# Decode attention in a hybrid decoder step: each partition subtracts its own maximum, the maximum across partitions is taken once per step, and the decode blocks pass two at a time

## What is computed

```python
def fox_attention(q, k, v, cq, ck, q_pos, k_pos):
    ...
        s = jnp.einsum('bqhd,bkhd->bhqk', q_blk, k,
                       preferred_element_type=jnp.float32) * scale
        s = s + (cq_blk[..., :, None] - ck_t[:, :, None, :])
        mask = k_pos[None, :] <= p_blk[:, None]
        s = jnp.where(mask, s, NEG_BIG)
        p = jax.nn.softmax(s, axis=-1)
        return jnp.einsum('bhqk,bkhd->bqhd', p.astype(v.dtype), v)
```

## Time and profile before

| | us |
|---|---|
| median of 3 runs | 1908.2 |
| lowest and highest | 1907.0, 1912.0 |
| the profiled execution | 1911.6 |
| its span, first to last instruction | 1910.0 |
| `fox` in it | about 130 to 745 |

### The profile page before, as it was taken

The page is one execution under the profiler, slowest core; times in us unless marked ns, Lnnn a source line. Parts: engine busy times, 40 slices in busy tenths (PEclk is TensorE's granted clock), DMA queues, the critical chain, the costliest instruction groups (busy, mean ns, idle before and its releaser), DMA issues. The chain is left out here.

```text
span 1910.0 us, 30732 instructions
## 1 busy us (share of the span) xinstructions
PE 1664.6 (87%) x10909; PEld 1571.7 (82%) x10909; DVE 933.8 (49%) x1794; ACT 684.5 (36%) x1089; POOL 541.0 (28%) x340
## 2 busy tenths in 40 slices
PE   4498797898799653898994999999999999999997
PEld 4487686787688532896993999999999999999997
DVE  6425537646646554537324545444444444544444
ACT  3323543553453441224234333222222222445344
POOL 4411222232223111623300222222222222544541
PEclk6699999899899865998996999999999999999999
DMA  3324244244243224400005431111111111211122
GB/s 102 117 75 133 70 136 137 80 135 134 67 145 115 69 96 160 175 1 25 23 1 216 133 100 44 44 44 47 52 44 44 44 49 50 106 51 45 45 67 89
DMA packets 211045, 158.16 MB, mean 83 GB/s; under 512 B 23201, under 2 KB 199233, under 8 KB 209872
## 3 DMA queue, kind: packets, MB, share of 16 engines
q1 hardware_dynamic: 168492, 120.48, 20.3%
q10 hardware_dynamic: 41656, 31.92, 5.5%
q0 software_dynamic: 784, 4.31, 0.6%
HBM read 123.95 MB, written 32.89 MB: 82 GB/s over the span
## 5 line engine op out<-in xcount | busy, mean ns | idle before, releaser
L176 PE MATMUL ps<-x_hi,w_hi 128*128 128x344 f32 x1584 | 508.3, 321 | 1.1 <-issue 1.1
L177 PE MATMUL ps<-x_lo,w_hi 128*128 128x344 f32 x1584 | 505.7, 319 | 0.0
L178 PE MATMUL ps<-x_hi,w_lo 128*128 128x344 f32 x1584 | 505.6, 319 | 0.0
L176 PEld LDWEIGHTS ps<-x_hi,w_hi 128*128 128x128 f32 x1584 | 297.6, 188 | 3.0 <-issue 1.4
L178 PEld LDWEIGHTS ps<-x_hi,w_lo 128*128 128x128 f32 x1584 | 298.0, 188 | 0.0
L177 PEld LDWEIGHTS ps<-x_lo,w_hi 128*128 128x128 f32 x1584 | 297.3, 188 | 0.1
L176 PE MATMUL ps<-h_hi,wm_hi 128*128 128x344 f32 x672 | 226.8, 337 | 0.2
L177 PE MATMUL ps<-h_lo,wm_hi 128*128 128x344 f32 x672 | 218.7, 325 | 0.0
L178 PE MATMUL ps<-h_hi,wm_lo 128*128 128x344 f32 x672 | 218.4, 325 | 0.0
L2284 POOL TENSOR_TENSOR w_lo<-w_raw,w_hi 128x1024 fp32r<-128x1024 f32 x42 | 110.1, 2621 | 371.2 <-ACT w_hi L2452 371.2
L2288 POOL TENSOR_TENSOR w_lo<-w_raw,w_hi 128x512 fp32r<-128x512 f32 x44 | 112.1, 2554 | 134.7 <-ACT w_hi L2495 134.7
(11 more groups left out here) (366 smaller groups left out, 2908.7 us busy)
## 6 DMA issues: line engine op xcount, KB each, us to landing
w_raw<-in_w_up SPq DMA_DIRECT2D x44, 512.0 KB, 3.9
k_past<-in_cache_k SPq DMA_DIRECT2D x256, 64.0 KB, 1.9
v_past<-in_cache_v SPq DMA_DIRECT2D x256, 64.0 KB, 2.0
wm_raw<-in_w_in ACTq DMA_DIRECT2D x28, 512.0 KB, 4.1
w_raw<-in_w_down SPq DMA_DIRECT2D x44, 256.0 KB, 2.7
gdn_scratch<-conv ACTq DMA_DIRECT2D x12, 528.0 KB, 3.1
g_qkv<-gdn_scratch SPq DMA_DIRECT2D x12, 528.0 KB, 9.9
x_scratch<-xT POOLq DMA_DIRECT2D x1, 4128.0 KB, 11.4
```

Source lines behind the costliest of these rows:

```text
L176: pe.matmul(out, w_hi, a_hi, start=first, stop=False)
L177: pe.matmul(out, w_hi, a_lo, start=False, stop=False)
L178: return pe.matmul(out, w_lo, a_hi, start=False, stop=last)
```

## The change

The subtraction of the maximum across partitions is taken out of each block. Each partition ("lane") subtracts its own maximum over the 8 pages (`lane_max`) right after the scores, in the same slot; the exponential follows in the same slot, the weighing one slot later, the page sums two slots later, into a tile `v_sum` that keeps the sums of all eight sequences of a step. In slot 0 of the next step POOL takes one maximum across partitions, 16 columns wide; DVE turns it into a factor for each lane, head and sequence (`factor_logs`), ACT exponentiates these factors (`exp_factors`, slot 1), DVE multiplies the lanes' sums of probabilities with them (`lane_weights`, slot 2), and PE sums over partitions in nine matmuls (`past_values`, slot 2): one for the denominators, and one for each sequence whose weights are `v_sum` and whose two columns are the factors. `dec_result` in slot 3 reads them from PSUM. `v_past` has 2 buffers instead of 3, and SP's load of a block waits for the page sums two blocks back.

The diff without the declarations of tiles and semaphores:

```diff
@@ fox: tiles
-        v_past = sb("v_past", [P, 3, PAGES, P])
+        v_past = sb("v_past", [P, 2, PAGES, P])
+        v_sum = sb("v_sum", [P, DEC, P])
...
@@ SP
             def load_v(n, pages):
-                need(sp, dval_done, 0, n - 2)
+                need(sp, v_summed, 0, n - 1)
                 settle(sp, "sp")
-                load_past(n, v_past[:, n % 3], t["cache_v"], pages, v_loaded[n % 3])
+                load_past(n, v_past[:, n % 2], t["cache_v"], pages, v_loaded[n % 2])
...
@@ PE
-            def past_values(n):
-
-                need(pe, v_summed, 0, n + 1)
-                need(pe, dval_out, 0, n)
-                if n % DEC == DEC // 2:
-                    need(pe, normed, n // DEC, 1)
-                pe.matmul(ps[:, 7, 0:16], v.ones[:], score[:, n % DEC].rearrange("p g h -> p (g h)"), start=True, stop=True)
-                pe.matmul(ps[:, 7, 16:17], v_past[:, n % 3, 0], v.ones[:, 0:1], start=True, stop=True).then_inc(dval_done.sem, 1)
+            def past_values(j):
+
+                need(pe, den_ready, j, 1)
+                need(pe, v_summed, j, DEC)
+                need(pe, normed, j, 1)
+                pe.matmul(ps[:, 7, 0:2 * DEC], v.ones[:], lane_sum.rearrange("p b h -> p (b h)"), start=True, stop=True)
+                for b in range(DEC):
+                    mm = pe.matmul(ps[:, 7, 2 * DEC + 2 * b:2 * DEC + 2 * b + 2], v_sum[:, b], lane_factor[:, b], start=True, stop=True)
+                mm.then_inc(dval_done.sem, 1)
...
                 l2_sums(j, i, 1)
-                if NBLK * j + i >= VALUES_AFTER:
-                    past_values(NBLK * j + i - VALUES_AFTER)
+                if j and i == 2:
+                    past_values(j - 1)
                 turn_probs(j, i, 1)
...
@@ ACT
                 need(act, dsub_ready, 0, n + 1)
-                act.activation(score[:, b], score[:, b], ACT.Exp)
-                act.activation(d_pself[:, j % 2, b], d_self[:, j % 2, b], ACT.Exp).then_inc(dexp.sem, 1)
+                act.activation(score[:, b], score[:, b], ACT.Exp).then_inc(dexp.sem, 1)
+
+            def exp_factors(j):
+                need(act, fsub_ready, j, 1)
+                act.activation(factors, factors, ACT.Exp).then_inc(factors_ready.sem, 1)
...
                         slot(j, i)
-                    n = NBLK * j + i - 1
-                    if 0 <= n < PAST:
-                        exp_decode(n)
+                        exp_decode(NBLK * j + i)
+                    if j and i == 1:
+                        exp_factors(j - 1)
...
@@ POOL
-            def all_max(n):
-                b = n % DEC
-                need(pool, dmax_ready, 0, n + 1)
+            def all_max(j):
+                need(pool, dsub_ready, j, DEC)
                 settle(pool, "pool")
-                pool.partition_all_reduce(d_all[:, b], d_max[:, b], P, RMAX).then_inc(dmax_all.sem, 1)
+                pool.partition_all_reduce(d_all.rearrange("p b h -> p (b h)"), lane_max[:, j % 2].rearrange("p b h -> p (b h)"), P, RMAX).then_inc(dmax_all.sem, 1)
...
                     n = NBLK * j + i
-                    if 0 <= n - 1 < PAST:
-                        all_max(n - 1)
+                    if j and i == 0:
+                        all_max(j - 1)
...
-                    if 0 <= n - 2 < PAST:
-                        weigh(n - 2)
+                    if 0 <= n - 1 < PAST:
+                        weigh(n - 1)
...
@@ DVE
-                dve.tensor_reduce(d_max[:, b], score[:, b].rearrange("p g h -> p h g"), AX.X, ALU.max).then_inc(dmax_ready.sem, 1)
-
-            def dec_less_max(n):
-                j, b = divmod(n, DEC)
-                need(dve, dmax_all, 0, n + 1)
-                dve.tensor_tensor(d_max[:, b], d_all[:, b], d_self[:, j % 2, b], ALU.max)
+                top = lane_max[:, j % 2, b]
+                dve.tensor_reduce(top, score[:, b].rearrange("p g h -> p h g"), AX.X, ALU.max)
                 dve.drain()
-                dve.tensor_tensor(score[:, b], score[:, b], d_max[:, b].unsqueeze(1).broadcast_to([P, PAGES, 2]), ALU.subtract)
-                dve.tensor_tensor(d_self[:, j % 2, b], d_self[:, j % 2, b], d_max[:, b], ALU.subtract).then_inc(dsub_ready.sem, 1)
+                dve.tensor_tensor(score[:, b], score[:, b], top.unsqueeze(1).broadcast_to([P, PAGES, 2]), ALU.subtract).then_inc(dsub_ready.sem, 1)
 
             def sum_pages(n):
 
                 need(dve, v_weighed, 0, n + 1)
-                vb = v_past[:, n % 3]
...
-            def past_out(n):
-                need(dve, dval_done, 0, n + 1)
-                b = n % DEC
-                dve.tensor_copy(dden[:, 16 * b:16 * b + 16], ps[:, 7, 0:16])
-                dve.tensor_copy(dnum[:, b:b + 1], ps[:, 7, 16:17]).then_inc(dval_out.sem, 1)
+                need(dve, dval_done, n // DEC, 0)
+                vb = v_past[:, n % 2]
...
+                dve.tensor_tensor(v_sum[:, n % DEC], vb[:, 0], vb[:, 1], ALU.add).then_inc(v_summed.sem, 1)
+
+            def lane_sums(j):
+                need(dve, dexp, j, DEC)
+                dve.tensor_reduce(lane_sum, score.rearrange("p b g h -> p b h g"), AX.X, ALU.add)
+
+            def factor_logs(j):
+                need(dve, dmax_all, j, 1)
+                dve.tensor_tensor(d_all, d_all, d_self[:, j % 2], ALU.max)
+                dve.drain()
+                dve.tensor_tensor(lane_factor, lane_max[:, j % 2], d_all, ALU.subtract)
+                dve.tensor_tensor(self_factor, d_self[:, j % 2], d_all, ALU.subtract).then_inc(fsub_ready.sem, 1)
+
+            def lane_weights(j):
+                need(dve, factors_ready, j, 1)
+                dve.tensor_tensor(lane_sum, lane_sum, lane_factor, ALU.mult).then_inc(den_ready.sem, 1)
...
                         normalise(j - 1)
+                        lane_sums(j - 1)
+                    if j and i == 2:
+                        lane_weights(j - 1)
                     if j < STEPS:
                         dec_score(j, i)
...
-                    if 0 <= n - 1 < PAST:
-                        dec_less_max(n - 1)
-                    if 0 <= n - VALUES_AFTER < PAST:
-                        past_out(n - VALUES_AFTER)
-                    if 0 <= n - 3 < PAST:
-                        sum_pages(n - 3)
+                    if 0 <= n - 2 < PAST:
+                        sum_pages(n - 2)
...
-                    if i == 3 and j:
+                    if j and i == 0:
+                        factor_logs(j - 1)
+                    if j and i == 3:
                         dec_result(j - 1)
```

More of the change, by code:

```diff
@@ L825, in fox @@
         score = sm(2 * DEC * PAGES).rearrange("p (b g h) -> p b g h", b=DEC, g=PAGES)
-        dden = sm(2 * DEC * PAGES)
-        d_max, d_all, d_den = (sm(2 * DEC).rearrange("p (b h) -> p b h", b=DEC) for _ in range(3))
-        d_self, d_pself = (sm(4 * DEC).rearrange("p (n b h) -> p n b h", n=2, b=DEC) for _ in range(2))
-        qk_self, dnum, d_tmp = sm(DEC), sm(DEC), sm(DEC)
+        lane_sum, d_all, d_den = (sm(2 * DEC).rearrange("p (b h) -> p b h", b=DEC) for _ in range(3))
+        d_self, lane_max, factors = (sm(4 * DEC).rearrange("p (n b h) -> p n b h", n=2, b=DEC) for _ in range(3))
+        lane_factor, self_factor = factors[:, 0], factors[:, 1]
+        qk_self, d_tmp = sm(DEC), sm(DEC)
         q_dec, k_dec = sm(DEC), sm(DEC)
@@ L849, in fox @@
         k_loaded = [count(f"kpast_loaded{i}", 0) for i in range(2)]
-        v_loaded = [count(f"vpast_loaded{i}", 0) for i in range(3)]
-        k_used, dmax_ready, dmax_all, dsub_ready, dexp = (count(n, DEC) for n in ("kpast_used", "dmax_ready", "dmax_all", "dsub_ready", "dexp"))
-        v_weighed, v_summed, dval_done, dval_out = (count(n, DEC) for n in ("v_weighed", "v_summed", "dval_done", "dval_out"))
+        v_loaded = [count(f"vpast_loaded{i}", 0) for i in range(2)]
+        k_used, dsub_ready, dexp, v_weighed, v_summed = (count(n, DEC) for n in ("kpast_used", "dsub_ready", "dexp", "v_weighed", "v_summed"))
+        dmax_all, fsub_ready, factors_ready, den_ready, dval_done = (count(n, 1) for n in ("dmax_all", "fsub_ready", "factors_ready", "den_ready", "dval_done"))
         dec_out, dec_stored = count("dec_out", 1), count("dec_stored", 16)
@@ L1391, in sum_pages @@
-                for m in (4, 2, 1):
-                    ins = dve.tensor_tensor(vb[:, 0:m], vb[:, 0:m], vb[:, m:2 * m], ALU.add)
-                    if m > 1:
-                        dve.drain()
-                ins.then_inc(v_summed.sem, 1)
-            def past_out(n):
-                need(dve, dval_done, 0, n + 1)
-                b = n % DEC
-                dve.tensor_copy(dden[:, 16 * b:16 * b + 16], ps[:, 7, 0:16])
-                dve.tensor_copy(dnum[:, b:b + 1], ps[:, 7, 16:17]).then_inc(dval_out.sem, 1)
@@ L1403, in dec_result @@
-            def dec_result(j):
-                need(dve, dexp, j, DEC)
-                dve.drain()
-                dve.tensor_reduce(d_den, dden.rearrange("p (b g h) -> p b h g", b=DEC, g=PAGES), AX.X, ALU.add)
-                dve.drain()
```

(7 more changed lines are left out.)

20 lines of the change are left out of this document (11 added, 9 removed).

## The result

The changed kernel takes 1880.1 us (median of 4 runs, 1875.8 to 1886.0) beside 1908.3 for the kernel before: 0.986 of it (95% interval 0.984 to 0.988), by this ratio 27 us faster. I had forecast 1830 and a range from 1803 to 1866, so the sign is right and the size is not: the change brought a third of the 78 us. Another run of the same kernel gave 0.985 (0.983 to 0.987).

What follows compares the result with a forecast made beforehand. GpSimd's queue, filled by all-reduces of 13.5 us, was taken to pace VectorE and through it a nearly full TensorE. Terms -50 - 19 + 5 - 2 - 12 = -78 us gave 1830 us, range 1803 to 1866.

Steps and rivals of the forecast that it cites:

- Item 1: TensorE's waits for VectorE's probabilities copy and score rounds, 58.2 us in the four steps, mostly go: -50 us (-58 to -43).
- the first places: Slots 2 to 3 of each step, where TensorE waits for copy and score round; 2 us left at each of four.
- the second ones: Slots 4 to 5 of each step, the other place of TensorE's waits for VectorE; nothing left there.
- Item 2: Seven stretches of TensorE work at half clock, 42.9 us, return to 2.4 GHz: -19 us (-21 to -10).
- Item 3: TensorE's l2 sums, reached earlier, wait longer for ScalarE's squares in half of the places: +5 us (0 to +10).
- Item 4: Values' matmuls within the steps fall from 10 to 6 us; about half lost to the transpose's copy wait: -2 us.
- Item 5: Tail after step 3: one all-reduce in line instead of three, decode result earlier: -12 us (-16 to -8).
- the signs that I had named: Prediction wrong if first-place holes stay above 5 us, GpSimd waits for values' loads, or all-reduce results take over 10 us.
- The unknown call: The all-reduce over 16 columns, not in the trace: taken at 13.5 us as for 2 columns; upper bound 108 us.
- The slower rival: The all-reduce grows with its columns; at 108 us a call the kernel takes 2190 us; chance 0.04.
- VectorE takes GpSimd's place: VectorE, about as full as TensorE in slots 1 to 3, binds; items 1 and 2 give 36: 1863 us; chance 0.20.
- the ring of two: With two values buffers loads come too late in short slots; GpSimd waits, 45 us given back: 1875 us; chance 0.04.

Runs made afterwards that it cites:

- after_again: The changed kernel itself, nothing altered, run again for comparison with other kernels on the same chip; 0.985 of the kernel before.
- no_reads: Changed kernel with GpSimd's weighing, weight split and mask tile all replaced by fills of the same tiles; 0.960 of the kernel before.
- no_reduce: Changed kernel with its four remaining all-reduces replaced by a GpSimd copy of 16 columns; 0.981 of the kernel before.
- v_first: Changed kernel with SP issuing a block's values ahead of the keys two blocks on instead of behind them; 0.981 of the kernel before.
- weigh_memset: Changed kernel with GpSimd filling a block's values with ones where it weighed them; 0.971 of the kernel before.

## Why the prediction was wrong

**What bounds the kernel.** Right: TensorE's idle time and clock are what could be won, and GpSimd's queue did pace VectorE. The release came: VectorE's 88.0 us of waiting are gone.

**Item 1, -50.** This term failed. Copy and score rounds together went from 62.1 to 27.2 us. Without the tail's 3.9, which item 1 left out, that is from 58.2 to 27.2 us, -31. At the first places, where I had left 2 us each, TensorE waits 5.8, 1.2, 3.8 and 3.8 us (step 0's hole had been 4.3 us, not the 10.7 that I took for all, and grew); at the second ones, where I had left nothing, 3.1 to 3.2 us in every step. The step that failed is the one with which I gave "nothing at the second ones" and 2 us at the first: I took VectorE's durations from rows in which GpSimd was in the silent stretch of an all-reduce (taps 4.09, sums 1.55) and kept them for a GpSimd that no longer stands still. The second place of step 1 shows it. Before, it was 3.0 us:

```profile
367.78 1.65 PE L967 MATMUL ps<-kT,qT 64*128 64x384 f32 x4 [3.04 <-DVE fox_small L1342]
```

After, it is 3.06 us, and VectorE's sums ahead of it take 3.18 and 1.84 us instead of 1.55 in all, beside split and weighing:

```profile
346.05 3.18 DVE L1391 TENSOR_TENSOR v_past<-v_past 128x512 f32<-128x512 f32 x2
349.30 1.84 DVE L1393 TENSOR_TENSOR v_sum<-v_past 128x128 f32<-128x128 f32 x1
...
346.30 2.64 POOL L730 TENSOR_TENSOR wm_lo<-wm_raw,wm_hi 128x1024 fp32r<-128x1024 f32 x1 [11.31 <-ACT wm_hi L726]
348.90 2.08 POOL L1302 TENSOR_TENSOR v_past<-v_past,fox_small 128x1024 f32<-128x1024 f32 x1
...
356.93 0.92 PE L967 MATMUL ps<-kT,qT 64*128 64x384 f32 x4 [3.06 <-DVE fox_small L1345]
```

Without GpSimd's reads the two waits are 7.3 us, -51: the size that I had.

**Item 2, -19.** TensorE was busy 10 us less in this profile and 0.6 less in that of `after_again`, at the same idle time (91.0 and 89.3); in `no_reads` 23 less, which is what items 2 and 4 take off its busy time together (19 and 4). The clock comes back where the holes go, and here half of them stayed.

**Item 3, +5.** It was +0.7, after and in `no_reads`. **Item 4, -2.** The wait of the transposes for their copies, which I had called half lost, grew from 13.2 to 20.3 us, and the collected matmuls wait 5.2 us in slot 2 of steps 1 to 3, where I had named the cover and priced it at nothing: together 12 us more, of which my sum had 2.

**Item 5, -12.** Right in size: from the start of the last decode scores to the next stage 35.1 us instead of 48.0, from their end to the decode result 28.7 us, where I had said 28: the end of the last block's subtraction and of the result's last product are

```profile
674.57 0.17 DVE L1383 TENSOR_TENSOR fox_small<-fox_small 128x16 f32<-128x16 f32 x1
...
703.25 0.16 DVE L1424 TENSOR_TENSOR fox_small<-fox_small 64x8 f32<-64x8 f32 x1
```

The all-reduce in it is worth less than I thought (3.6 us, `no_reduce`).

**The sum.** This profile is 36 us shorter instead of 78: item 1 brought 19 us too little, TensorE's busy time (items 2 and 4) 13, and the waits of item 4 took 10 more than I had; item 3 came out 4 us better, and the next stage lost 4. Two of the signs that I had named came: a first place above 5 us, in step 0, and GpSimd waiting for the values' loads.

**The unknown call.** The all-reduce over 16 columns has about the cost of the one over 2, as taken; my estimate of 1.7 us more for the columns does not show in the recorded part (0.39 us for 0.37):

```profile
419.51 0.39 POOL L1307 PARTITION_ALL_REDUCE fox_small<-fox_small  x1 [5.96 <-issue]
```

Behind the four calls 6.8 to 7.7 us follow without a record. The slower rival is out.

**The rivals.** "VectorE takes GpSimd's place" was the right one, with "if sums and weighings collide more than now" as its condition; it had 0.20 and a time of 1863. It was too low in both, since I priced only the first places. The condition stood in my own rows: the product with the keys takes 1.22 us in one slot and 2.01 in the next, with no other shape; the second one begins while a weight split still runs, and the weighing behind that split takes 2.88 instead of 1.89 us:

```profile
313.93 2.38 POOL L730 TENSOR_TENSOR wm_lo<-wm_raw,wm_hi 128x1024 fp32r<-128x1024 f32 x1
316.27 2.88 POOL L1298 TENSOR_TENSOR v_past<-v_past,fox_small 128x1024 f32<-128x1024 f32 x1
```

I read these rows for VectorE's load and not for the difference. Of the ring of two the wait came, 105.5 us in 13 slots instead of the 45 that I had, in part by SP's order (68.6 in `v_first`). But `weigh_memset` has that wait too and is 27 us faster: by itself it cost little. That it set the weighings beside taps and sums is read from the timelines and not shown by a run.

Shown, by leaving out, by filling and by moving, is that the reads of the weighing and of the split cost some 38 of the 50 us that are missing (27 and 11). Another 10 go with the mask tile, the zeros or the shorter split; that is open. That `no_reads` lands within 2 us of my forecast is partly luck: the transposes wait 7 us longer there than before, where I had counted 2, and against it stand a tail of 31.7 us, 16 less instead of 12, and squares that cost 4 us less than I took.

## What to carry to other kernels

An engine that waits much can be keeping out of the way of the others; before its waits are taken away, ask which of its operations will then run beside which, and take durations for the sum from rows where both are at work. When one shape shows two durations in a trace, find out what ran beside the longer one before using the shorter. Two engines that disturb one another can be put behind one another by a wait, where the second then has something to run beside that does not disturb it: here waits in four slots of each step were worth 25 us, nearly as much as the change.

## What the runs showed of the hardware

In these traces GpSimd's operations that read SBUF and VectorE's operations with two operands there exclude one another whole: an addition of 0.29 us took 2.33, a tap of 1.32 took 2.79, a mask tile of 0.7 took 1.75. VectorE's score rounds, which take one operand from PSUM, kept their time beside GpSimd: 0.685 us on average for those of 512 columns, before and after. Beside GpSimd's fills 2 to 5 us of stretch remain; in `no_reads` they lie mostly on VectorE's small copies within SBUF (one of 8 columns takes 0.37 us on average there, 0.16 before).

The Trainium skill (SBUF — State Buffer, SBUF: two separate sides) calls this an exclusive lock, held by whichever instruction starts first until it ends. The timelines of slot 1 agree in both directions.

The same kernel can have TensorE 469.9 or 479.5 us busy in the stage at the same idle time: the profile of the change had the clock at 0.92 there, the other at 0.91. A difference of 10 us in TensorE's busy time between two single profiles so says nothing of a change by itself; the ratios in the table come from several runs of each.
